# Order of pieces and loads in three layers, memory rows in columns 256 to 511, and a residual turned in halves within the value tiles, in a transformer kernel on one Trainium2 core

## The reference, cut to what matters

```
# first block
u = rmsnorm(h, g);  y = dilated_mixer(u)          # three groups of windows, 16 heads each
u = rmsnorm(h, g);  y = diff_mixer(u)             # 8 heads, softmax(q1 k1) - lambda * softmax(q2 k2)
# second block, for l in (0, 1):
u = mlstm_rglru_mixer(rms_norm(h))                # l = 0
u = sliding_window_sink_attention(rms_norm(h))    # l = 1
h = h + rms_norm(u, g_mix_post[l])
u = memory_cross_attention(rms_norm(h, g_x_pre[l]), mem, g_mem[l], w_q, w_kv, w_o)
h = h + rms_norm(u, g_x_post[l])
h = h + rms_norm(squared_relu_mlp(rms_norm(h), w1, w2), g_ff_post[l])

def memory_cross_attention(u, mem, ...):
    q = u @ w_q;  k, v = split(rms_norm(mem) @ w_kv)     # 4 heads of 256
    return (softmax(q k^T * 256 ** -0.5) v) @ w_o
```

## Time and profile before

| | us |
|---|---|
| median of 3 runs | 2508.92 (2507.97 to 2510.13) |
| the profiled execution | 2509.11 |
| its span, first to last instruction | 2507.3 |
| mean granted TensorE clock | 0.983 of full |

### The profile page before, as it was taken

One profiled execution on the slowest core, in us unless ns is written; L12 is line 12 of the kernel. 1 busy time (PEld: TensorE's weight loads), 2 busy tenths in 40 slices (PEclk: granted clock), 3 DMA queues, 4 the chain that ended last, 5 costly groups with the idle time before them and its releaser, 6 DMA issues.

```text
span 2507.3 us, 40093 instructions
## 1 busy us (share of the span) xinstructions
PE 2387.8 (95%) x13062; PEld 1947.0 (78%) x13062; DVE 1198.5 (48%) x2375; ACT 1107.2 (44%) x2396; POOL 1028.1 (41%) x750
## 2 busy tenths in 40 slices
PE   7999999999999889998999999999898999999998
PEld 6787888787877668666878888888766878888886
DVE  4555555554677753575344622223785424522224
ACT  5433333345544545553644632323565634523232
POOL 4444444442533324441651444443422742544442
PEclk9999999999999989998999999999999999999999
DMA  5333333332322213221431232332322421332332
GB/s 188 112 98 98 96 99 95 105 102 85 110 85 84 84 51 92 65 79 53 128 111 47 93 99 94 92 99 77 93 64 81 136 92 51 101 101 93 97 92 79
DMA packets 126065, 231.99 MB, mean 93 GB/s; under 512 B 17120, under 2 KB 17248, under 8 KB 125920
## 3 DMA queue, kind: packets, MB, share of 16 engines
q1 hardware_dynamic: 123072, 219.56, 29.1%
q10 hardware_dynamic: 2848, 10.49, 1.2%
HBM read 208.48 MB, written 2.10 MB: 84 GB/s over the span
## 4 chain that ended last, share of the span: by engine, by line
issue 54%; PE 22%; POOL 22%; ACT 1%; POOLq 1%; DVE 1%; ACTq 0%; DMA 0%; DVEq 0%; SPq 0%
POOL wl L401 22%; PE PS L430 20%; PE PS L499 1%; PE PS L511 0%; POOLq L400 0%; PE PS L468 0%; POOLq L409 0%; ACT wh L1077 0%; PE PS L458 0%; PE PS L506 0%; ACTq L1087 0%; DMA raw<-tiles_dram 0%; ACT work L1106 0%; DVE ul L1697 0%; DVE ul L1706 0%
## 5 line engine op out<-in xcount | busy, mean ns | idle before, releaser
L401 POOL TENSOR_TENSOR wl<-raw,wh 128x512 fp32r<-128x512 f32 x746 | 1027.9, 1401 | 1451.6 <-ACT wh L1077 1450.3
L430 PE MATMUL PS<-uh,wh 128*128 128x512 f32 (+1 forms) x2120 | 798.6, 377 | 23.0 <-DVE ul L1706 8.6
L430 PE MATMUL PS<-uh,wl 128*128 128x512 f32 (+1 forms) x2120 | 782.4, 369 | 0.0
L430 PE MATMUL PS<-ul,wh 128*128 128x512 f32 (+1 forms) x2120 | 781.7, 369 | 0.0
L1077 ACT ACTIVATE wh<-raw 128x512 fp32r<-128x512 f32 x746 | 430.4, 623 | 349.7 <-PE PS L430 279.3
L430 PEld LDWEIGHTS PS<-uh,wh 128*128 128x128 f32 x2120 | 402.8, 190 | 111.1 <-issue 19.5
L430 PEld LDWEIGHTS PS<-uh,wl 128*128 128x128 f32 x2120 | 402.5, 190 | 67.6
L430 PEld LDWEIGHTS PS<-ul,wh 128*128 128x128 f32 x2120 | 403.1, 190 | 62.8 <-issue 0.8
L430 PE MATMUL PS<-wh,hid_sb 128*128 128x512 f32 x1024 | 322.0, 396 | 0.0
L1225 ACT ACTIVATE work<-PS 128x512 f32<-128x512 f32 (+1 forms) x156 | 89.7, 575 | 354.8 <-PE PS L430 281.4
L430 PEld LDWEIGHTS PS<-wh,hid_sb 128*128 128x128 f32 x1024 | 192.4, 188 | 46.2
(11 more groups left out here) (224 smaller groups left out, 2413.6 us busy)
## 6 DMA issues: line engine op xcount, KB each, us to landing
raw<-tiles_dram SPq DMA_DIRECT2D x746, 256.0 KB, 2.7
work<-work SPq DMA_DIRECT2D x296, 64.0 KB, 2.0
gB<-post_dram ACTq DMA_DIRECT2D x8, 512.0 KB, 3.7
H<-x_dram SPq DMA_DIRECT2D x4, 512.0 KB, 6.3
H<-x_dram ACTq DMA_DIRECT2D x4, 512.0 KB, 6.7
work<-mem_dram ACTq DMA_DIRECT2D x2, 1024.0 KB, 6.2
out_dram<-H ACTq DMA_DIRECT2D x4, 512.0 KB, 2.6
cst<-consts_dram SPq DMA_DIRECT2D x1, 644.0 KB, 5.1
```

The lines of the kernel that those rows point to most:

```text
L401: nc.gpsimd.tensor_tensor(w_of(wl, slot)[:, hc], raw[:, s, hc], w_of(wh, slot)[:, hc].bitcast(F32), ALU.subtract).then_inc(lo_ready, 1)
L430: last = nc.tensor.matmul(out, a, b, start=start and m == 0, stop=stop and m == 2)
```

## The change

Seven places change; L numbers are of the kernel before.

1. `first_tiles`: the last twelve matmuls of the first half (features 4 to 7 of the fourth tile) come after the transposes of rows 2 and 3. The wait for the former layer's evacuations stands before the transposes, as before.
2. `last_tokens` of a begun projection: PE's pieces of rows 0 and 1 in the order (0,1), (0,2), (1,0), (1,1), (1,2), (0,3), (1,3), so that the last tile comes last. It was (0,1), (0,2), (0,3), (1,0) to (1,3).
3. `dil_out`: the four loads of `x` into `H` are issued one, one and two behind the splits of three tiles, and no longer all before them.
4. `diff`: DVE takes the maximum of unit 2 within `diff_norm`, before the steps of its inverse root, and scales the former head's result after the weights of unit 2. `frden` is double. The last stage does `split_lo(0, 2)`; in `diff_last` the begun pieces, the outputs of head 6 and the norm of head 6 stand elsewhere.
5. `ev_out` and `sw_out`: memory rows are written to `xn` rows 2 and 3 and columns 256 to 511 (`at=2`, `MEM_FORTH`, `MOVED_MEM`), and the residual's rows are taken in the order 2, 3, 0, 1.
6. `cross`: rows 0 and 1 of the residual are turned between the two value blocks, rows 2 and 3 within the first four query tiles, which run in halves of 256 columns. ACT takes the four square sums ahead of the splits of tiles b+11 to b+14, and makes `uh` in halves.
7. `sw`: each quarter stands one unit earlier, two ahead of the first scores.

```diff
-        PLAIN, MOVED = [0, 1, 2, 3, 4, 5, 6, 7], [0, 1, 7, 2, 3, 4, 5, 6]
+        PLAIN, MOVED, MOVED_MEM = [0, 1, 2, 3, 4, 5, 6, 7], [0, 1, 7, 2, 3, 4, 5, 6], [0, 1, 7, 2, 5, 6, 3, 4]
+        CROSS, QUERY = [0, 1, 6, 7, 0, 1, 6, 7], [2, 3, 4, 5]
+        FORTH, MEM_FORTH = (0, 1, 2, 3), (2, 3, 0, 1)
...
-        DIFF_EARLY = early(6) + [(1, 0, k) for k in range(6)] + [(0, t, 7) for t in range(TT)]
+        DIFF_EARLY = [(0, t, k) for k in range(2) for t in range(2)] + [(0, 2, 0), (0, 2, 1)] + early(6)[6:24]
+        DIFF_EARLY += [(1, 0, k) for k in range(4)] + [(0, t, 6) for t in range(TT)]
+        DIFF_EARLY += [(1, 0, 4), (1, 0, 5)] + [(0, t, 7) for t in range(TT)]
...
-                half_tiles(n, 0, u0, banks)
+                half_tiles(n, 0, u0, banks, [(0, 0, KT), (1, 0, KT), (2, 0, KT), (3, 0, 4)])
                 pe.wait_ge(taken, c.get("out") if evacuated is None else evacuated)
-                half_tiles(n, 1, half_transposes(1, banks), banks)
+                u1 = half_transposes(1, banks)
+                half_tiles(n, 0, u0, banks, [(3, 4, KT)])
+                half_tiles(n, 1, u1, banks)
...
-                for t in range(2):
-                    for j in range(0 if t else begun // 2, 4):
-                        if t == 0:
-                            pe.wait_ge(lo_ready, 2 * (n + j + 1))
-                        last = piece(t, j)
-                    last.then_inc(bank_done, 1)
+            def last_tokens(n, piece, turn_rows, begun=0, order=FORTH):
+
+                if begun:
+                    pieces = [(0, j) for j in range(begun // 2, 3)] + [(1, 0), (1, 1), (1, 2), (0, 3), (1, 3)]
+                else:
+                    pieces = [(t, j) for t in range(2) for j in range(4)]
+                for t, j in pieces:
+                    if t == 0:
+                        pe.wait_ge(lo_ready, 2 * (n + j + 1))
+                    last = piece(order[t], j)
+                    if j == 3:
+                        last.then_inc(bank_done, 1)
...
-                    tok_block(n, slot_of(n), KT, [2 + 2 * nb, 3 + 2 * nb])
-                pe.wait_ge(lin_evac, L0 + 8)
-                u0 = norm_transposes(TT, late_k=2, late=c.add("out", 4))
-                for m in range(8):
-                    n = b + 16 + m
-                    feature_tile(n, slot_of(n), m % 2, L0 + 8 + m, first_u=u0 if m == 0 else None)
+                    tok_block(n, slot_of(n), KT, [2 + 2 * nb, 3 + 2 * nb], t0=2)
+                    if nb == 0:
+                        pe.wait_ge(lin_evac, L0 + 8)
+                        u0 = half_transposes(0, CROSS)
+                n, copied = b + 16, c.add("out", 4)
+                pe.wait_ge(y_copied, copied - 2)
+                half_tiles(n, 0, u0, QUERY, [(0, 0, KT), (1, 0, KT)])
+                pe.wait_ge(y_copied, copied)
+                half_tiles(n, 0, u0, QUERY, [(2, 0, KT), (3, 0, 4)])
+                u0 = half_transposes(1, CROSS)
+                half_tiles(n, 0, u0, QUERY, [(3, 4, KT)])
+                half_tiles(n, 1, u0, QUERY)
+                for m in range(4, 8):
+                    feature_tile(n + m, slot_of(n + m), m % 2, L0 + 8 + m)
...
+                if between is not None:
+                    between(-2)
+                    between(-1)
                 unit_scores(0)
                 unit_scores(1)
-                if between is not None:
-                    between(-1)
...
+                    if again:
+                        for t in ((0,), (1,), (2, 3))[j - 2]:
+                            act.dma_start(H[:, t, :], x[t * P:(t + 1) * P, :]).then_inc(x_in[t], 16)
...
-                for m in range(8, 11):
-                    split_g(b + m + 3)
+                act.wait_ge(h_tile, c.add("h", TT))
                 for t in range(TT):
-                    norm_squares(H, [t])
-                    split_g(b + 11 + t + 3)
-                split_g(b + 15 + 3)
-                norm_hi(("g_x_pre", 8 * l), TT)
+                    norm_squares(H, [t], waits=False)
+                    split_g(b + 11 + t)
+                half_hi(("g_x_pre", 8 * l), 0, CROSS)
+                for m in range(15, 20):
+                    split_g(b + m)
+                half_hi(("g_x_pre", 8 * l), 1, CROSS)
                 for m in range(8):
-                    split_g(b + 16 + m + 3)
-                    take(b + 16 + m, xq(m), m % 2)
+                    if m:
+                        split_g(b + 16 + m + 3)
+                    take(b + 16 + m, xq(m), QUERY[m] if m < 4 else m % 2)
...
                 v.tensor_scalar(g.bitcast(I32), g.bitcast(I32), -1.0, 1597463007.0, ALU.mult, ALU.add)
+                if between is not None:
+                    between()
...
-                        diff_norm(A - 1, par)
-                    diff_max(A, 2)
+                        diff_norm(A - 1, par, between=lambda: diff_max(A, 2))
+                    else:
+                        diff_max(A, 2)
+                    diff_weights(A, ap, 2)
                     if former:
                         diff_scaled(A - 1, par)
-                    diff_weights(A, ap, 2)
-                diff_rotate(L, 1, par, between=None if A is None else lambda: diff_max(A, 3))
+                diff_rotate(L, 1, par, between=None if A is None else lambda: last_max(L, A))
+
+            def last_max(L, A):
+
+                diff_max(A, 3)
+                if isinstance(L, int) and L == 7:
+                    split_lo(0, 2)
...
+                norm_rows(H, range(2))
...
-                        norm_rows(H)
-                norm_lo(("g_x_pre", 8 * l))
+                        half_lo(("g_x_pre", 8 * l), 0, CROSS)
+                        norm_rows(H, range(2, TT))
+                half_lo(("g_x_pre", 8 * l), 1, CROSS)
...
-                    if n < 23:
-                        quarter(n + 1)
+                    if n < 22:
+                        quarter(n + 2)
                         return
```

More of the change, by code:

```diff
@@ L512, in chain, with tok_block @@
                 return last
-            def tok_block(n, slot0, K, banks, u0=None, free=None, rows=None):
+            def tok_block(n, slot0, K, banks, u0=None, free=None, rows=None, t0=0):
                 xh, xl = rows or (uh, ul)
@@ L1143, in last_tokens @@
             def last_tokens(b, square, gain, mem_of=None, banks=PLAIN):
-                for t in range(2):
+                order = FORTH if mem_of is None else MEM_FORTH
+                for t in order[0:2]:
                     square(t)
@@ L1656, in step, with rsqrt @@
                 v.drain()
-            def rsqrt(out, var, n):
+            def rsqrt(out, var, n, between=None):
                 g, t, w = stat[:, 12:12 + n], stat[:, 16:16 + n], stat[:, 60:60 + n]
```

146 lines of the change are left out of this document (72 added, 74 removed).

## The result

The changed kernel takes 2484.78 us (median of 4, 2483.3 to 2486.81), against 2509.14 for the kernel before on the same chip: a ratio of 0.9901, interval 0.9887 to 0.9915. That is 24.4 us where 33.5 were forecast; the time lies within the range, 9 us above the value predicted. A few executions on record fell into a slower state of the chip (3365.55 us, for one) and are left out of every number here. The profiled execution has a span of 2484.1, 23.2 less than in the earlier trace rows.

The account below looks back on a forecast made before the run. TensorE bound it, busy 2387.8 of 2507.3 us, so only idle and low-clock time could go. Terms summed to 37.1, less 2.7 for clock and 0.9 for shifted waits, 33.5: 2509.1 to 2475.6 us, range 2461 to 2490.

Parts of the forecast that it names:

- Parts 1 and 2: Five first_tiles handovers: waits for ul covered, 7.1 us; differential attention loop: six waits for unit 2's weights gone, 8.4 us.
- Part 3: Last heads of diff: two of three ul waits and the loop's leftover wait go, 5.9 us, bounds 3 and 7.6.
- the others, 5.2, go: At the last heads, the ul waits other than the last feature's 2.35 us one disappear, worth 5.2 us.
- Parts 4 and 5: Turns of dil_out and diff_out: late last tile covered, row chain sets the gain, 3.4 and 1.7 us.
- I put it 4.3 us earlier: At dil_out, interleaving the loads of x brings the last weight tile 4.3 us earlier, from ACT's 6.12 us wait.
- The clock stretch, taken at 0.8: Turns of dil_out and diff_out: two new low-clock stretches, 1.7 us each at chance 0.8, 2.7 lost in all.
- Part 6: Two cross attentions: waits for xn and ul covered by value blocks, net gain 3.2 us in x0, 4.9 in x1.
- The 1.3 us for split query tiles: Cross attentions: four query tiles in halves turn 96 matmuls of 512 into 192 of 256, 1.3 us added each time.
- Part 7: Sliding window: two quarters moved ahead of the first scores gain 2.5 us, between 1.4 and 4.4.
- They hide 2.7 of them: Sliding window: the two quarters ahead of the first scores cover 2.7 of those scores' 3.18 us wait.
- rival (C): Whole kernel slower: the weight chain of load, ACT split and POOL low half sets the pace; 2515 us, chance 0.03.
- the signs that I named: No ul waits over 0.3 at second halves, none at unit 2; idle down 28 to 33, clock up 0.003 or less.

Follow-up runs that it names:

- the old order alone: The changed kernel with the former order of pieces, (0,1) to (0,3) then (1,0) to (1,3), in all three begun projections: 2477.9 us, ratio 0.9886.
- the old order with late loads and fill: The changed kernel with the former piece order, loads of x behind the third split, ten identity transposes ahead of the first normed row: 2478.66 us.
- the fill alone: The changed kernel with 16 and 10 identity transposes ahead of the two normed-row waits at the turns of dil_out and diff_out: 2478.73 us.

## Why the prediction came out as it did

- **Parts 1 and 2** were right in mechanism and size: 7.1 forecast and 7.0 measured alone, 8.4 forecast and 7.8 measured alone (9.1 within the loop). The rule of the Trainium skill, page "SBUF — State Buffer", section "SBUF: two separate sides", on the shared port pair, set beside the weights' operation, was not tested at that place. In the window its sign recurs: 2.54 us for the pair of L2375 beside POOL, where the median of one such operation in the window is 0.35.
- **Part 3**, 5.9 forecast, came out at 6.4, the elapsed time from head 6's last scores to the first piece on the last head's feature (51.5 before, 45.2 after, for the same instructions), and part of that is luck. PE's idle in it fell only from 10.9 to 7.3. The step that failed is "the others, 5.2, go": 1.7 of the first wait is still there, and where four waits for the low half held 1.3 us, one now holds 3.0. One slow stretch of the clock fewer (1.7 by the price used) and some shorter busy time made up for it; neither was in the sum.
- **Parts 4 and 5**, 5.1 less 2.7 for the clock. The waits at the turns came as forecast in kind and somewhat longer (2.43 and 1.71; 2.1 and 1.7; 3.2 in all was forecast for the first turn). The failed step is "I put it 4.3 us earlier": two of the four loads were still issued ahead of the tile, ACT waited 5.11 and not 1.8, and with none ahead the time that ACT needs to issue the four stood in the way, a term that the sum didn't have. The clock stretch, taken at 0.8, came at both turns. Beside the 1.46 of the first tiles, the net was 0.2 gained at `dil_out`, and 0.8 lost at `diff_out` (99.1 us from the last head's feature to a fixed point in `ev` before, 98.5 after).
- **Part 6** was right: 3.3 and 5.0 against 3.2 and 4.9. POOL at 75% was no bound in `x1`. The 1.3 us for split query tiles can be read from the changed kernel: in `x0` 84 of them in a row take 10.07 us, 0.120 each, and 192 x 0.120 less 96 x 0.227 is 1.3.

```profile
1250.21 0.28 PE L440 MATMUL PS<-uh,wh 128*128 128x256 f32 x1
...
1260.28 1.91 PE L474 MATMUL PS<-cst,work 128*128 128x128 f32 x16
```

The estimate of 0.24 that the prediction took from the Trainium skill, page "TensorE: Matmul & The Clock Gate", section "Back-to-back issue gap", is too low here; the measurement decides.
- **Part 7** had the wrong sign, and it is the largest part of the miss. "They hide 2.7 of them" was nearly true (3.18 became 1.05), and I left it there, with the wait at the start as the whole account. I never asked who sets the pace behind it. DVE does (26.59 us busy of 33), so what PE wins ahead of the scores it waits for again. And I took the quarter as free where it came from: late in the window it was the only filler, without it two waits of 1.4 and 1.0 became one of 3.4 and the clock fell to 0.81 of full. Alone, the edit costs 4.3 us (2.3 to 6.5) where 2.5 were forecast as gained, which would be 6.8 of the 9 missed; taken back in the changed kernel it returns 1.9, which is within the spread and would make it 4.4. The window's stretch as a whole is 7.7 short of the forecast, and 3.3 of that is there with the quarters back in their place, for a wait and a slow stretch whose cause is open. I had named the mechanism, as rival (C), for the weight chain, and not for the engine that has it here.
- Of the 1.1 lost before the first scores, 0.9 is not the change: after the start's 2.2 us wait the clock stayed low for eleven matmuls in one execution and for seven in the other.
- Of the signs that I named, no wait on `ul` over 0.3 us is left at the five second halves, and the unit 2 waits of the loop are gone but one of 0.4. But PE's idle fell by 24.7 us and not by 28 to 33, and the granted clock did not rise: 0.982 against 0.983.

What stays open: the spread of 3 us between executions of one kernel (and 10 in one of them) goes with the granted clock (0.006 of its mean for those 10), so differences under 3 us between the variants are not settled by their medians. The fastest, the old order alone (2477.9), the old order with late loads and fill (2478.66) and the fill alone (2478.73), are equal within that.

## What to carry to other kernels

Here a wait covered at the head of a loop did not pay, because the loop's pace was not PE's: before counting such a wait, look at the busy share of the engine on the other side of the handover in the loop's windows. Filler moved forward is filler taken away, so price both ends. Where PE must stand for a few microseconds, a few matmuls that compute nothing can be worth as much as an earlier result, since a lower clock outlasts the wait. And a load moved out of the way of the transfers costs the engine that issues it: look at what stands behind it in that engine's queue.

## What the runs showed of the hardware

- Two idles, 2.43 and 1.71 us, with 1.06 us of transposes between them, were followed by nine matmuls at half the rate; the same two shortened by fillers to 1.34 and 0.69 were followed by none. Idles of 2.3 and 1.4 us with 16 us of work between (the old order of pieces) brought no fall at this place either, though at `diff_out` in the same profile a single idle of 2.35 us was followed by a stretch at the lower level. By the Trainium skill, page "TensorE: Matmul & The Clock Gate", section "What's actually happening", the clock is set by how busy the array was just before, and how many matmuls run slow differs from run to run; both agree with what is seen here (eleven and seven at the same place at the start).
- Two VectorE scalings of 128x256 took 2.54 us together beside two GpSimd operations of 2.54 together, against 0.35 each as the median of the window.
- Issuing four loads of 512 KB in a row kept ScalarE from its next operation for 2.07 us (2.65 from the first issue to the end of the last).
- On a queue that carries both weight loads and exchanges between partitions, moving only the work that releases the loads made the exchanges late: VectorE waited 19.5 us for them in six places, TensorE 22.9 behind it, and the kernel took 25 us longer.
